# Prompt and samples convolved in one row, first tap and kept columns on ScalarE, head selectors read from the identity

## The reference

```python
SSM_HEADS, SSM_HEAD_DIM, SSM_GROUPS, SSM_STATE, SSM_CONV_K = 32, 64, 4, 128, 4
SSM_D_INNER, SSM_CONV_DIM = 2048, 3072

def causal_dwconv(u, hist, w):
    k_width = w.shape[0]
    t_len = u.shape[1]
    full = jnp.concatenate([hist.astype(u.dtype), u], axis=1)
    y = sum(w[j] * full[:, j:j + t_len] for j in range(k_width))
    return y, full[:, t_len:]

def mamba2_mixer(h, conv_hist, ssm_state, ...):
    z, xbc, dt = jnp.split(h @ w_in, [SSM_D_INNER, SSM_D_INNER + SSM_CONV_DIM], axis=-1)
    xbc, new_conv_hist = causal_dwconv(xbc, conv_hist, conv_w)
    xbc = jax.nn.silu(xbc + conv_b)
    ...
    y, new_state = ssd_scan(x, dt, a, b, c, ssm_state)   # states decay by exp(dt * a) per head
```

## Time and profile before

| | |
|---|---|
| median of 3 runs | 1121.42 us (1121.11 to 1121.51) |
| the profiled execution's own time | 1120.12 us |
| its span | 1118.3 us |
| TensorE busy | 1040.0 us (93%) |
| VectorE busy | 721.0 us (64%) |
| ScalarE busy | 481.7 us (43%) |
| GpSimd busy | 48.6 us (4%) |

### The profile page before, as it was taken

The page is one execution under the profiler, slowest core; times in us unless marked ns, Lnnn a source line. Parts: engine busy times, 40 slices in busy tenths (PEclk is TensorE's granted clock), DMA queues, the critical chain, the costliest instruction groups (busy, mean ns, idle before and its releaser), DMA issues.

```text
span 1118.3 us, 21486 instructions
## 1 busy us (share of the span) xinstructions
PE 1040.0 (93%) x8659; PEld 950.3 (85%) x8659; DVE 721.0 (64%) x1357; ACT 481.7 (43%) x807; POOL 48.6 (4%) x93
## 2 busy tenths in 40 slices
PE   5899999889889999999899997889999899999996
PEld 3899888534589999999789997777889799999995
DVE  4544668655458665644598999677984676666344
ACT  4332444232355443443455632464663544344341
POOL 4000400000000000000000002021000000000000
PEclk9899999978799999999999999799899899999998
DMA  9375999999953545444434563089225355454501
GB/s 290 114 248 165 282 349 347 348 348 348 337 175 118 184 152 174 157 161 153 149 114 151 153 186 115 1 253 325 66 86 163 102 162 178 152 182 139 179 29 42
DMA packets 194100, 206.15 MB, mean 184 GB/s; under 512 B 8232, under 2 KB 186621, under 8 KB 193951
## 3 DMA queue, kind: packets, MB, share of 16 engines
q1 hardware_dynamic: 173714, 178.54, 50.1%
q10 hardware_dynamic: 16816, 15.25, 4.4%
q0 software_dynamic: 3472, 10.99, 3.2%
HBM read 192.59 MB, written 12.17 MB: 183 GB/s over the span
## 4 chain that ended last, share of the span: by engine, by line
PE 74%; DVE 16%; ACT 4%; DMA 3%; ACTq 1%; issue 1%; SPq 0%; POOL 0%; DVEq 0%
PE acc L794 18%; PE acc L796 17%; PE acc L795 17%; DVE WHL L1771 4%; PE trb L877 3%; PE scb L898 3%; PE acc L877 2%; PE scb L1010 2%; DVE Z L2222 2%; DVE RR L1748 1%; PE scb L767 1%; ACT WHL L1357 1%; DVE X L2157 1%; DMA ring<-in_state_ssm_dram 1%; DMA ring<-in_cache_v_dram 1%
## 5 line engine op out<-in xcount | busy, mean ns | idle before, releaser
L794 PE MATMUL acc<-HX,WHL 128*128 128x288 f32 x928 | 280.7, 302 | 18.7 <-DVE HX L1760 14.7
L795 PE MATMUL acc<-HX,WHL 128*128 128x288 f32 x928 | 277.3, 299 | 0.0
L796 PE MATMUL acc<-HX,WHL 128*128 128x288 f32 x928 | 276.8, 298 | 0.0
L1357 ACT ACTIVATE WHL<-ring 128x1024 fp32r<-128x1024 f32 (+1 forms) x140 | 138.9, 1040 | 178.0 <-PE acc L796 178.0
L1771 DVE TENSOR_TENSOR WHL<-ring,WHL 128x1024 fp32r<-128x1024 f32 (+1 forms) x140 | 163.2, 1206 | 74.2 <-ACT WHL L1357 74.2
L794 PEld LDWEIGHTS acc<-HX,WHL 128*128 128x128 f32 x928 | 178.1, 192 | 22.9 <-issue 18.7
L795 PEld LDWEIGHTS acc<-HX,WHL 128*128 128x128 f32 x928 | 179.5, 193 | 0.2
L796 PEld LDWEIGHTS acc<-HX,WHL 128*128 128x128 f32 x928 | 179.2, 193 | 0.0
L1357 ACT ACTIVATE W<-ring 128x1024 fp32r<-128x1024 f32 x84 | 82.7, 1032 | 130.6 <-PE acc L796 130.6
L1771 DVE TENSOR_TENSOR W<-ring,W 128x1024 fp32r<-128x1024 f32 x84 | 97.1, 1197 | 54.1 <-ACT W L1357 54.1
L794 PE MATMUL acc<-HX,W 128*128 128x288 f32 x352 | 105.8, 301 | 5.5 <-DVE HX L1760 5.1
(11 more groups left out here) (406 smaller groups left out, 1853.8 us busy)
## 6 DMA issues: line engine op xcount, KB each, us to landing
ring<-in_l_w_in_dram SPq DMA_DIRECT2D x32, 1024.0 KB, 5.3
ring<-in_l_ffn_gate_dram SPq DMA_DIRECT2D x22, 1024.0 KB, 5.2
ring<-in_l_ffn_up_dram SPq DMA_DIRECT2D x22, 1024.0 KB, 5.3
ring<-in_l_ffn_down_dram SPq DMA_DIRECT2D x16, 1024.0 KB, 5.1
Z<-in_cache_k_dram SPq DMA_DIRECT2D x52, 256.0 KB, 7.7
ring<-in_cache_k_dram SPq DMA_DIRECT2D x52, 256.0 KB, 7.6
Z<-in_cache_v_dram SPq DMA_DIRECT2D x48, 256.0 KB, 8.0
ring<-in_cache_v_dram SPq DMA_DIRECT2D x48, 256.0 KB, 7.4
```

The lines of the kernel that those rows point to most:

```text
L794: pe.matmul(out, w[:, 0, at:at + P], part_at(k, 0), start=(k == 0), stop=False)
L795: pe.matmul(out, w[:, 0, at:at + P], part_at(k, 1), start=False, stop=False)
L796: last = pe.matmul(out, w[:, 1, at:at + P], part_at(k, 0), start=False, stop=(k == kdim - 1))
L1357: act.activation(split_weights(i)[:, 0, half], ring[:, slot_of(u), half], ACT.Copy).then_inc(w_hi, 1)
```

## The change

Prompt and samples of a chunk now lie in one row `ext` of 315 columns: 3 + 256 of the prompt, then 8 groups of 3 history and 4 new columns. One multiply-add per tap runs over 312 columns, also over those between sequences, whose results nobody reads. The first tap is done by ScalarE into a double-buffered `CONV` (`first_taps`), as are the samples' histories and the kept columns; VectorE does the other three taps (`other_taps`). ScalarE's SiLU of a pair (`silu_pair`) reads `CONV`, is held back by one unit and stands behind that unit's split and first taps. New semaphores: `hist_set`, `tap_made` (ScalarE to VectorE, one per chunk), `ext_read` (ScalarE has read `ext`, so VectorE may fill it again). `conv_samples` is gone. The table `E2` is gone, with GpSimd's two instructions: `spread_head` takes one column of the identity, repeated 64 times, as the stationary operand, and writes 64 rows of the bank, one matmul per head where there was one per two heads.

```diff
-        exts = Area(Z, a.at).take(CC, NB, T + 3)
-        EXTMP = Area(flat(Y)).take(CC, NB, T)
+        EXT_P, EXT_S = NP + 3, NB * (T + 3)
+        EXT = EXT_P + EXT_S
+        CONV = Area(Z, a.at).take(2, 2, EXT)
...
-            step(pool.memset(E2[0:SH, :, :], 0.0))
-            step(pool.affine_select(out=E2[0:SH, :, :].rearrange("p k (q r) -> p k q r", q=2),
...
-            pe.wait_ge(xc_made, CC + 2)
+            pe.wait_ge(xc_made, 2 * CC)
...
+            def spread_head(out, h, of_heads):
+                half = slice(h % 2 * DH, (h % 2 + 1) * DH)
+                return pe.matmul(out[half, :], ident[0:SH, h:h + 1].to_broadcast([SH, DH]), of_heads, start=True, stop=True)
+
             bank = acc_open()
-            pe.wait_ge(consts, marks["e2"])
-            for k in range(CX):
-                last = pe.matmul(bank[:, k * (NB + 1):(k + 1) * (NB + 1)], E2[0:SH, k, :], decin[:, :], start=True, stop=True)
+            for h in range(SH):
+                k = h // 2
+                last = spread_head(bank[:, k * (NB + 1):(k + 1) * (NB + 1)], h, decin[:, :])
...
-                for k in range(CX):
+                for h in range(SH):
+                    k = h // 2
                     at = (k % PG * G + k // PG) * NS
-                    last = pe.matmul(bank[:, at:at + NS], E2[0:SH, k, :], hw[:, 1, NP:NT], start=True, stop=True)
+                    last = spread_head(bank[:, at:at + NS], h, hw[:, 1, NP:NT])
...
+            def first_taps(pair, n, free_at):
+                act.wait_ge(cv_made, 2 * n)
+                act.activation(ext[:, :, EXT_P:].rearrange("p e (b t) -> p e b t", t=T + 3)[:, :, :, 0:3],
+                               hists[:, 2 * pair:2 * pair + 2, :].rearrange("p e (b j) -> p e b j", j=3), ACT.Copy).then_inc(hist_set, 1)
+                act.wait_ge(hist_set, n + 1)
+                act.wait_ge(acc_free, free_at)
+                for e in range(2):
+                    c = 2 * pair + e
+                    act.activation(CONV[:, n % 2, e, 0:EXT - 3], ext[:, e, 0:EXT - 3], ACT.Copy,
+                                   scale=par[:, 1, c:c + 1]).then_inc(tap_made, 1)
+                cs = slice(2 * pair, 2 * pair + 2)
+                act.activation(co_s[:, cs, 0:3], ext[:, :, NP:NP + 3], ACT.Copy)
+                for e in range(2):
+                    last = act.activation(co_s[:, 2 * pair + e, 3:].rearrange("p (b j) -> p b j", j=3),
+                                          of_samples(ext[:, e, EXT_P:])[:, :, T:T + 3], ACT.Copy)
+                last.then_inc(ext_read, 1)
+
+            def silu_pair(pair, n):
+                for e in range(2):
+                    c = 2 * pair + e
+                    act.wait_ge(cv_made, 2 * n + e + 1)
+                    bias = par[:, 0, PCB + c:PCB + c + 1]
+                    act.activation(XBC[:, c, 0:NP], CONV[:, n % 2, e, 0:NP], ACT.Silu, bias=bias).then_inc(xc_made, 1)
+                    act.activation(XBC[:, c, NP:NT].rearrange("p (b t) -> p b t", t=T), of_samples(CONV[:, n % 2, e, EXT_P:])[:, :, 0:T],
+                                   ACT.Silu, bias=bias).then_inc(xc_made, 1)
...
                 if kind == "c":
-                    for c in (2 * i, 2 * i + 1):
-                        n_cv += 1
-                        act.wait_ge(cv_made, n_cv)
-                        act.activation(XBC[:, c, 0:NP], XBC[:, c, 0:NP], ACT.Silu,
-                                       bias=par[:, 0, PCB + c:PCB + c + 1]).then_inc(xc_made, 1)
-                    if n_cv == CC:
-                        silu_samples(2, 0, CX)
+                    first_taps(i, n_pairs, acc_in1(pos) + 2)
+                if held is not None:
+                    silu_pair(*held)
+                    held = None
+                if kind == "c":
+                    held = i, n_pairs
+                    n_pairs += 1
...
-            def conv_taps(pair):
+            def other_taps(pair, n):
                 dve.wait_ge(acc_free, n_acc[0])
-                dve.tensor_copy(co_s[:, 2 * pair:2 * pair + 2, 0:3], ext[:, :, NP:NP + 3])
                 made = [None, None]
-                for j in range(4):
+                for j in range(1, 4):
                     for e in range(2):
                         c = 2 * pair + e
...
+                        dst = CONV[:, n % 2, e, 0:EXT - 3]
+                        if j == 1:
+                            dve.wait_ge(tap_made, 2 * n + e + 1)
                         else:
                             dve.wait_ge(vch, made[e])
...
-            def conv_samples(first, last):
...
                 if kind == "c":
-                    if n_cv:
-                        dve.wait_ge(cv_made, n_cv)
+                    if n_pairs:
+                        dve.wait_ge(cv_made, 2 * n_pairs)
+                        dve.wait_ge(ext_read, n_pairs)
                     conv_input(2 * i)
                     conv_input(2 * i + 1)
```

More of the change, by code:

```diff
@@ L236, in hybrid_decoder_kernel @@
         XDS = q.take(DI)
-        E2 = q.take(CX, P)
         CE1 = Area(Z, AT_L1 + (CC + CX) * NT).take(2, HG * DH)
@@ L355, in hybrid_decoder_kernel @@
         cv_made = sem("cv_made")
-        cvs_made = sem("cvs_made")
+        hist_set = sem("hist_set")
+        tap_made = sem("tap_made")
+        ext_read = sem("ext_read")
         xc_made = sem("xc_made")
@@ L1590, in dt_function, with of_samples @@
                 act.activation(dst, src, func, scale=scale).then_inc(dt_act, 1)
[L1592 to L1597, removed]
+            def of_samples(t):
+                return t.rearrange("p (b t) -> p b t", t=T + 3)
+            def first_taps(pair, n, free_at):
[22 more added lines that the diff above has]
+                                   ACT.Silu, bias=bias).then_inc(xc_made, 1)
+            n_pairs, held = 0, None
             for pos, (kind, i) in enumerate(IN1):
@@ L1620, in _ @@
                     act.activation(ZS[:, 2 * i:2 * i + 2, :], ZS[:, 2 * i:2 * i + 2, :], ACT.Silu).then_inc(zs_made, 1)
-                if pos == Z_UNITS[5]:
-                    silu_samples(1, CX, CC)
+            act.wait_ge(ext_read, n_pairs)
+            act.sem_inc(co_made, 1)
             def mask_b(b):
@@ L2203, in conv_input @@
                 bank = take()
-                new = exts[:, c, :, 3:]
-                dve.tensor_tensor(ext[:, e, 3:], bank[:, 0:NP], RR[:, 0:NP], ALU.mult)
+                new = ext[:, e, EXT_P:].rearrange("p (b t) -> p b t", t=T + 3)[:, :, 3:]
+                dve.tensor_tensor(ext[:, e, 3:EXT_P], bank[:, 0:NP], RR[:, 0:NP], ALU.mult)
                 free(dve.tensor_tensor(new, bank[:, NP:NT].rearrange("p (b t) -> p b t", t=T),
                                        RR[:, NP:NT].rearrange("p (b t) -> p b t", t=T), ALU.mult))
-            def conv_taps(pair):
+            def other_taps(pair, n):
                 dve.wait_ge(acc_free, n_acc[0])
-                dve.tensor_copy(co_s[:, 2 * pair:2 * pair + 2, 0:3], ext[:, :, NP:NP + 3])
                 made = [None, None]
-                for j in range(4):
+                for j in range(1, 4):
                     for e in range(2):
                         c = 2 * pair + e
[L2216 to L2219, removed]
+                        dst = CONV[:, n % 2, e, 0:EXT - 3]
+                        if j == 1:
+                            dve.wait_ge(tap_made, 2 * n + e + 1)
                         else:
                             dve.wait_ge(vch, made[e])
-                            ins = dve.scalar_tensor_tensor(dst, src, tap, dst, ALU.mult, ALU.add)
+                        ins = dve.scalar_tensor_tensor(dst, ext[:, e, j:j + EXT - 3], par[:, 1, j * CC + c:j * CC + c + 1], dst,
+                                                       ALU.mult, ALU.add)
                         if j < 3:
@@ L2226, in conv_taps @@
                             ins.then_inc(cv_made, 1)
-            def conv_samples(first, last):
-                n = last - first
-                new = XBC[:, first:last, NP:NT].rearrange("p c (b t) -> p c b t", t=T)
-                def of_chunk(table, at):
-                    return table[:, at + first:at + last].unsqueeze(2).unsqueeze(3).to_broadcast([P, n, NB, T])
-                if first == 0:
-                    dve.tensor_copy(co_s[:, :, 3:].rearrange("p c (b j) -> p c b j", j=3), exts[:, :, :, T:T + 3]).then_inc(co_made, 1)
-                link(dve.tensor_tensor(new, exts[:, first:last, :, 0:T], of_chunk(par[:, 1, :], 0), ALU.mult))
-                for j in range(1, 4):
-                    link(dve.tensor_tensor(EXTMP[:, 0:n], exts[:, first:last, :, j:j + T], of_chunk(par[:, 1, :], j * CC), ALU.mult))
-                    link(dve.tensor_tensor(new, new, EXTMP[:, 0:n], ALU.add))
-                dve.tensor_tensor(new, new, of_chunk(par[:, 0, :], PCB), ALU.add).then_inc(cvs_made, 1)
             def dt_exponent():
@@ L2324, in _ @@
                 if kind == "c":
-                    conv_taps(i)
+                    other_taps(i, n_pairs)
+                    n_pairs += 1
```

(4 more changed lines are left out.)

10 lines of the change are left out of this document (2 added, 8 removed).

## The result

The changed kernel takes 1105.38 us (median of four executions, 1104.33 to 1107.07) against 1121.47 us: a ratio of 0.9849 (95% interval 0.9827 to 0.9872), 16.1 us less. The forecast was 1110.0 us with a range from 1106.5. The direction and the mechanism came as predicted; the gain is 4.6 us larger than the sum, and 1.1 us beyond the range.

A forecast was written before the change was run, and what follows sets the result against it. TensorE was taken to bound the projection, VectorE its end, with both selector groups on the path. Terms 0.7 + 5.8 + 1.1 + 1.5 + 1.7 + 0.6 = 11.4 us gave 1110.0 us, range 1106.5 to 1116.

The forecast's parts named there:

- B: TensorE's wait at the end of the layer-1 input projection: goes whole, 5.8 us saved, bounds 5.0 to 5.8.
- C: From L1097 to the first selector matmuls: fewer evictions ahead and faster transposes save 1.1 us, bounds 0.5 to 1.8.
- A: Inside the layer-1 input projection: the late stall goes and ScalarE's added work lies beside TensorE, 0.7 us saved.
- D: First selector group, as 32 matmuls in alternating halves: 1.5 us saved, bounds 0 and 2.0, passing on whole.
- E: Second selector group, in the same new form: 3.75 us against 2.05, 1.7 us saved, bounds 0 and 1.7.
- F: Work behind the second selector group until L2474: shortens if the clock stays up, 0.6 us, bounds 0 and 1.3.
- Rival 1: Selector groups: the new loads do not overlap, so D, E and F go, 7.6 us; 1113.8 us, chance 0.22.
- rival 3: Projection's end: another wait replaces the removed one, or the stage behind swallows the gain; 1114 to 1121 us, chance 0.06.
- Rival 2: Selector groups and state stage: clock stays up longer, C, D, F at upper ends; 15 us, 1106.4 us, chance 0.16.
- Rival 4: c units of the projection: ScalarE's new work delays VectorE through `tap_made` and the kernel gets slower; chance 0.03.
- limit of 8.05 us: Projection: length of VectorE's c chain up to which a z unit takes up lateness; beyond it each us costs 12.
- The signs named ahead: L1097's wait under 0.5 us, selector groups 2.0 to 2.6 us, clock 1.00 after the second, first taps within 4 us.

The follow-up runs named there:

- `first_only`: Kernel before, table `E2` kept, with only the first selector group read from the identity through `spread_head`: 1120.01 us, ratio 0.9979.
- `second_only`: Kernel before, table `E2` kept, with only the second selector group read from the identity through `spread_head`: 1116.72 us, ratio 0.9967.
- `heads_sorted`: Changed kernel with both selector groups' heads reordered, lower halves of the rows first, then upper: 1113.5 us, ratio 0.9904.

## Why the prediction was right in its mechanism and short in its size

- **B, 5.8 us: right.** The wait of 5.76 us is gone whole. That GpSimd's table was 1.53 us of its cause did not change the sum.
- **C, 1.1 us: right (1.18), but on a condition that the prediction had priced at nothing.** "GpSimd's two E2 instructions vanish, so the mask behind them is early" is worth 2.3 us in that stage alone (8.31 against 6.00): with the wait gone, the table would have been the next bound.
- **A, 0.7 us: 1.6 us, mis-sized by 0.9** (128.82 - 5.76 = 123.06 to L1097's wait, against 121.47). The prediction took the 0.58 us idle of the earlier trace rows as the cost of the stall. Before, the starts of matmuls show more:

```profile
685.63 0.37 PE L794 MATMUL acc<-HX,WHL 128*128 128x288 f32 x1 [0.58 <-DVE WHL L1771]
685.84 0.29 PE L795 MATMUL acc<-HX,WHL 128*128 128x288 f32 x1
685.97 0.29 PE L796 MATMUL acc<-HX,WHL 128*128 128x288 f32 x1
```

  The first of these starts 0.88 us after the one ahead of it, the second 0.21 us after that, and the usual pitch is 0.13: 0.83 us lost for 0.58 idle. Two such places, at 582.9 and 640.4, with 0.31 and 0.38 us, stood in no list of waits. Together 1.52 us, and in the changed kernel none of the three is left.
- **D, 1.5 us: 1.7 to 3.0 us** to the first turned state; the group itself is 2.0 us shorter, the predicted upper bound, and the spread is the clock behind it (L1123 above). That this "passes on whole" is not shown: `first_only` gained nothing that could be told from chance, and TensorE waits longer for the states' loads, 5.2 and 5.3 us in the profiles of after, 4.0 and 4.4 in those of before. The line of before, beside the first of the result's waits:

```profile
PE trb L1140 <- DMA ring<-in_state_ssm_dram: 4.0, 2, 2.9
```

- **E, 1.7 us: 1.70 us** in the first pair of profiles, as predicted, and 2.3 us against the second profile of before.
- **F, 0.6 us with a bound of 1.3: 2.0 to 3.0 us. This is the step that failed.** E and F together were to give 2.3 us, and the stage of the second group gave 3.7 to 5.3; `second_only`, which changes this group alone, gives the same 52.94 us, and `heads_sorted`, which takes only the alternation away, loses it again (58.20). F went wrong by its bound: "VectorE waited 1.3 us there, which is the most to be had". One wait of one engine is no bound on what the clock costs: at half clock TensorE itself was the path, and the windows above show it for over 8 us. The prediction had the row (0.50 behind the slow group, 1.00 behind L1233) and sized it by another.
- **Rival 1** fell (2.03 and 2.05 us), **rival 3** fell. **Rival 2** is in part what happened, and its 1106.4 us are the nearest of the times named: the clock stays up, but behind the second group and not in the state stage, where it still falls. **Rival 4** did not happen; its mechanism shows with 3.3 us more on ScalarE, and its limit of 8.05 us is not confirmed. The signs named ahead came, the first taps of the last c unit among them: done 3.3 us after its evictions begin (675.48 to 678.74).

The terms with their measured sizes are 1.6 + 5.8 + 1.2 + 1.7 to 3.0 + 3.7 to 5.3 = 14.0 to 16.9 us, and the measured 16.1 lies in it. That is in part luck, not a proof: between the first turned state and the second selector group the profiles of after are 0.3 to 5.9 us longer than those of before, behind the last column 0.7 to 1.1 us, and upstream 1.1 to 3.0 us shorter, all in code with the same instructions and with the clock's falls at other places each time. How these average over executions stays open, and so does how much of the 16.1 us is gained upstream or lost again in the states.

## What to carry to other kernels

Price a slow stretch on TensorE by the granted clock of the rows behind it, and by all the work that these hold, not by the wait of whoever reads the result. Count a stall from start to start. When a wait goes away, look for what else was hidden under it: a neighbour engine's work that cost nothing before can eat most of the gain.

## What the runs showed of the hardware that was not expected

- A group of matmuls that keeps TensorE "busy" all the time can lower its clock: over the table's second group the profile shows TensorE busy for 2.00 of 2.00 us, 19 matmuls in it, and the clock at 0.74 and then 0.50 over the next 10 us; 66 matmuls in the same time leave it at 1.00. This holds for the second group; behind the first the clock fell with alternating halves too, in six profiles of nine.
- Two copies of 32x8 elements took 1.60 us on VectorE beside a GpSimd instruction, 0.34 us without it.
- Executions of one kernel spread more than the first three suggested: 1116.3 to 1129.2 us for the kernel before on one core, where the first three had 1121.1 to 1121.5. In its two profiles the clock falls in other places behind the samples' own matmuls (5.26 and 6.89 us to the second group).
